# Down product of three MLP groups in four by Strassen's algorithm, weight sums by accumulating DMAs, last norm by column halves

## What is computed

```
for i in range(2):
    h = h + mixer_i(rms_norm(h, norm_mix_g[i]))
    h = h + square(relu(rms_norm(h, norm_mlp_g[i]) @ w_up[i])) @ w_down[i]
return rms_norm(h, norm_final_g)          # h: 512 x 1024
```

## Time and profile before

| | |
|---|---|
| runs, median | 1224.68 us |
| profiled execution, own time | 1224.22 us |
| its span | 1222.5 us |
| PE busy | 1195.8 us (98%), 5821 matmuls |
| DVE busy | 614.3 us (50%) |
| ACT busy | 457.5 us (37%) |
| Pool busy | 41.8 us (3%) |
| DMA | 119.00 MB, mean 97 GB/s |

### The profile page before, as it was taken

How to read it: one execution, slowest core, us unless ns; L and a number is a source line. 1 busy time by engine, 2 the same in 40 slices (tenths; PEclk the granted TensorE clock), 3 DMA queues, 4 the chain that set the end, 5 groups by cost and what they waited for, 6 DMA issues and landing times.

```text
span 1222.5 us, 14644 instructions
## 1 busy us (share of the span) xinstructions
PE 1195.8 (98%) x5821; PEld 1001.4 (82%) x5821; DVE 614.3 (50%) x838; ACT 457.5 (37%) x712; POOL 41.8 (3%) x88
## 2 busy tenths in 40 slices
PE   6999999999999999999999999999999999999996
PEld 5788888888888888888878988987888888888885
DVE  5447878645334344354357666574543433443432
ACT  6346676544223133133345224243531331331421
POOL 2000000000000000000020101100000000000001
PEclk9999999999999999999999999999999999999999
DMA  9245745523233322333211230133322333222101
GB/s 280 65 95 135 161 125 147 192 84 116 93 102 103 103 86 86 103 104 103 84 57 35 70 104 12 59 104 103 121 85 89 102 103 103 90 87 97 34 0 69
DMA packets 115991, 119.00 MB, mean 97 GB/s; under 512 B 38913, under 2 KB 84001, under 8 KB 115938
## 3 DMA queue, kind: packets, MB, share of 16 engines
q1 hardware_dynamic: 112992, 116.47, 31.4%
q10 hardware_dynamic: 2946, 1.79, 0.5%
HBM read 103.50 MB, written 2.10 MB: 86 GB/s over the span
## 4 chain that ended last, share of the span: by engine, by line
PE 95%; DVE 2%; ACT 1%; DMA 1%; issue 1%; POOL 0%; SPq 0%; POOLq 0%; ACTq 0%; DVEq 0%
PE bank L890 15%; PE bank L893 15%; PE bank L894 15%; PE bank L877 10%; PE bank L881 10%; PE bank L880 10%; PE bank L1064 2%; PE bank L1068 2%; PE bank L1067 2%; PE bank L1234 2%; PE bank L1112 2%; PE bank L1099 1%; PE bank L1185 1%; PE bank L1189 1%; PE bank L1188 1%; PE bank L1081 1%
## 5 line engine op out<-in xcount | busy, mean ns | idle before, releaser
L1427 DVE TENSOR_TENSOR w_lo<-w_stage,w_hi 128x2048 fp32r<-128x2048 f32 x87 | 199.9, 2300 | 204.1 <-ACT w_hi L559 204.0
L559 ACT ACTIVATE w_hi<-w_stage 128x2048 fp32r<-128x2048 f32 x87 | 165.9, 1910 | 267.2 <-PE bank L890 213.3
L877 PE MATMUL bank<-hT_lo,w_hi 128*128 128x512 f32 x512 | 199.8, 390 | 0.0
L881 PE MATMUL bank<-hT_hi,w_lo 128*128 128x512 f32 x512 | 199.3, 389 | 0.0
L890 PE MATMUL bank<-w_lo,u_hi 128*128 128x512 f32 x512 | 199.3, 389 | 0.0
L880 PE MATMUL bank<-hT_hi,w_hi 128*128 128x512 f32 x512 | 199.2, 389 | 0.0
L894 PE MATMUL bank<-w_hi,u_lo 128*128 128x512 f32 x512 | 199.2, 389 | 0.0
L893 PE MATMUL bank<-w_hi,u_hi 128*128 128x512 f32 x512 | 199.2, 389 | 0.0
L890 PE MATMUL bank<-w_lo,hT_hi 128*128 128x512 f32 (+1 forms) x320 | 115.1, 360 | 4.4 <-DVE hT_lo L1718 1.9
L1501 DVE TENSOR_TENSOR u_sq<-relu 128x512 f32<-128x512 f32 x64 | 44.3, 692 | 143.2 <-ACT relu L616 143.2
L616 ACT ACTIVATE relu<-bank 128x512 f32<-128x512 f32 x64 | 38.3, 598 | 205.3 <-PE bank L881 205.3
(11 more groups left out here) (206 smaller groups left out, 1513.8 us busy)
## 6 DMA issues: line engine op xcount, KB each, us to landing
w_stage<-in_mlp_w_up_dram SPq DMA_DIRECT2D x32, 1024.0 KB, 5.1
w_stage<-in_mlp_w_down_dram SPq DMA_DIRECT2D x32, 1024.0 KB, 5.0
w_stage<-in_fox_w_in_dram SPq DMA_DIRECT2D x32, 256.0 KB, 4.3
w_stage<-in_gla_w_in_dram SPq DMA_DIRECT2D x8, 1024.0 KB, 5.1
w_stage<-in_fox_w_in_dram SPq DMA_DIRECT2D x4, 1024.0 KB, 8.0
qa<-qk_hi SPq DMA_DIRECT2D x32, 128.0 KB
w_stage<-in_fox_w_out_dram SPq DMA_DIRECT2D x4, 1024.0 KB, 5.2
w_stage<-in_gla_w_in_dram SPq DMA_DIRECT2D x8, 512.0 KB, 4.4
```

The source lines that it names most:

```text
L559: act.activation(w_hi[:, slot, :], w_stage[:, slot, :], ACT.Copy).then_inc(w_hi_made, 1)
L877: a = pe.matmul(out, w[0][:, k, :], x[1][:, k, :], start=(k == 0), stop=False)
L881: a = pe.matmul(out, w[1][:, k, :], x[0][:, k, :], start=False, stop=(k == KT - 1))
L1427: dve.tensor_tensor(w_lo[:, slot, :], w_stage[:, slot, :], fp(w_hi[:, slot, :]), ALU.subtract).then_inc(w_lo_made, 1)
```

## The change

The order of the inner columns is used to cut a group's down product into quadrants. The group's u (512 tokens by 1024 inner columns) is seen as A11, A12, A21, A22 with 256 tokens each and the even or odd tiles of 128 inner columns (four of each); the weights (1024 by 1024) as W11, W12, W21, W22 of 512x512, one unit each. Three groups of four in each layer use seven products in place of eight (Winograd's form of Strassen's algorithm); the fourth is as before.

- The loop has 11 units: U0 to U3 for the up part, then W11, T1 = W11 + W12, T2 = T1 + W22, W22, T3 = W12 + W22, W21, T4 = T2 + W21. T1, T2 and T4 are made one after the other in stage slot 3, T3 in stage slot 1, each by a DMA issued on Pool that adds 1 MB from DRAM to what the slot holds (`weight_sums`). An add in slot 3 is issued when DVE has made the `lo` part of the slot's last value.
- Of u, `u_raw` holds the squares of two k blocks. DVE forms r1 = A21 - A22, s3 = A11 - A21, s2 = r1 - A11, s4 = A12 + s2 (`sums`, 256 columns each). ACT and DVE then make `hi` and `lo` of seven parts of 256 columns at once (`hi`, `lo`); for the fourth block in two pieces: A12, A22, A11 first, then r1, s2, s3, s4. A21 itself is not split.
- A product is 4 k blocks x 2 token blocks x 3 matmuls into two banks (`product`). `begins` is set for three of the seven; the other four go on top of a bank's content once DVE has collected it into `h` (`collect`, scaled by `mlp_scale` or `mlp_minus`). PE's first product waits at its first matmul until three of the four blocks have their `lo` parts, and the first two wait at their fourth k block for the last.
- The squares before the norm, the iota constants and the masks keep their content but move: `xor` and `other` lie in `gate_w`, the masks are made after the third group of layer 0.
- The last norm: ACT's squares of the left half come first, DVE multiplies the left half by the gain (`scale_left`) between the two halves' adds, ACT multiplies by `rstd` (`left`), and DVE does the right half of block t behind the add of block t+1 (`right`). The gain is loaded by ACT into `w_stage` in the last group. The last block is stored in two halves, by ACT and by SyncE.

Constants and order of units:

```diff
-GLA_U = MLP0_U + 8 * GROUPS
+WINO = GROUPS - 1
+WINO_UNITS = 11
+U0, U1, U2, U3, W11, T1, T2, W22, T3, W21, T4 = range(WINO_UNITS)
+HI_SLOT = (0, 1, 3, 1, 2, 0, 1, 2, 0, 1, 2)
+STAGE = (0, 1, 2, 0, 3, 3, 3, 0, 1, 2, 3)
+LEFT_FOR = (W21 - WINO_UNITS, T4 - WINO_UNITS, U0, U2, T4 - WINO_UNITS, U1, W11, T1, T2, W22, T3)
+WINO_LOADS = ((U0, 0, T3 - WINO_UNITS), (U1, 1, T3 - WINO_UNITS), (U2, 2, T4 - WINO_UNITS),
+              (W11, 3, T4 - WINO_UNITS), (U3, 0, U0), (T3, 1, U1), (W21, 2, U2), (W22, 0, U3))
+LOADS_PER_SLOT = (3, 2, 2, 1)
+A_R1, A_S2, A_S3, A_S4, A_12, A_22, A_11, A_21 = range(8)
+PRODUCTS = ((W11, A_11, 4), (T1, A_R1, 6), (T2, A_S2, 4), (W22, A_S4, 6), (T3, A_S3, 4), (W21, A_12, 2), (T4, A_22, 4))
+SUMS = ((0, 0, 1), (2, 1, 1), (0, 1, -1), (0, 1, 1), (2, 1, -1), (0, 0, 1), (2, 0, 1))
+HB = 2 * P
+CLASSIC0_U = MLP0_U + WINO * WINO_UNITS
+GLA_U = CLASSIC0_U + 8
 GLA_OUT_U = GLA_U + 3 * GLA_H
...
```

SyncE's loads and Pool's accumulating DMAs:

```diff
-                    load_rows(g, 8, c + 4, down_d[layer], g * KT)
+                with sp.Fori(0, WINO) as g:
+                    for unit, slot, free in WINO_LOADS:
+                        sp.wait_ge(w_lo_made, g * WINO_UNITS + (c + free + 1))
+                        if unit < 4:
+                            dma = sp.dma_start(cols(w_stage, slot, 256), up_d[layer][:, :, ds(g * D + unit * 256, 256)])
+                        else:
+                            two, half = {W11: (0, 0), T3: (0, 1), W21: (1, 0), W22: (1, 1)}[unit]
+                            dma = sp.dma_start(w_stage[:, slot, :].rearrange("p (k n) -> p k n", k=KT // 2),
+                                               down_pairs_d[layer][:, ds(g * (KT // 2), KT // 2), two,
+                                                                   half * S:(half + 1) * S])
+                        dma.then_inc(w_loaded[slot], 16)
...
@@ -462,7 +534,31 @@
                 pool.wait_ge(squared, n * 2 * TB + TB)
                 step(pool.tensor_tensor(ss[:, 0, :], ss[:, 0, :], ss[:, 1, :], ALU.add))
                 step(pool.tensor_tensor(ss[:, 0, :], ss[:, 0, :], mean_eps[:], ALU.add))
-                pool.tensor_tensor(mlp_scale[:], ss[:, 0, :], minus_one[:], ALU.pow).then_inc(mlp_scale_made, 1)
+                step(pool.tensor_tensor(mlp_scale[:], ss[:, 0, :], minus_one[:], ALU.pow))
+                pool.tensor_tensor(mlp_minus[:], mlp_scale[:], minus_one[:], ALU.mult).then_inc(mlp_scale_made, 1)
+
+            def weight_sums(layer):
+
+                c = (MLP0_U, MLP1_U)[layer]
+
+                def rows(g, two, half):
+                    return down_pairs_d[layer][:, g * (KT // 2):(g + 1) * (KT // 2), two, half * S:(half + 1) * S]
+
+                def add(slot, src, unit):
+                    pool.dma_start(w_stage[:, slot, :].rearrange("p (k n) -> p k n", k=KT // 2), src,
+                                   accum_op=ALU.add).then_inc(t_made[unit], 16)
+
+                for g in range(WINO):
+                    first = c + g * WINO_UNITS
+                    count, per, slot = wino_loaded(layer, T3)
+                    pool.wait_ge(w_loaded[slot], 16 * (g * per + count))
+                    add(1, rows(g, 1, 1), T3)
+                    pool.wait_ge(w_lo_made, first + W11 + 1)
+                    add(3, rows(g, 0, 1), T1)
+                    pool.wait_ge(w_lo_made, first + T1 + 1)
+                    add(3, rows(g, 1, 1), T2)
+                    pool.wait_ge(w_lo_made, first + T2 + 1)
+                    add(3, rows(g, 1, 0), T4)
 
             def gla_norm():
```

ACT's order in a group (`raw` is relu and square in place; `wino_hi` waits for `w_begun` and for the load or the sum):

```diff
+            def wino_hi(layer, g, unit):
+
+                c = (MLP0_U, MLP1_U)[layer]
+                act.wait_ge(w_begun, g * WINO_UNITS + (c + LEFT_FOR[unit] + 1))
+                if unit in (T1, T2, T3, T4):
+                    act.wait_ge(t_made[unit], g * 16 + 16 * (layer * WINO + 1))
+                else:
+                    count, per, slot = wino_loaded(layer, unit)
+                    act.wait_ge(w_loaded[slot], g * (16 * per) + 16 * count)
+                act.activation(w_hi[:, HI_SLOT[unit], :], w_stage[:, STAGE[unit], :], ACT.Copy).then_inc(w_hi_made, 1)
...
+                def raw(g, t):
+
+                    j, to = t // 2, raw_parts(t // 2, *((A_11, A_21 + 1) if t % 2 == 0 else (A_12, A_22 + 1)))
+                    act.wait_ge(up_done, g * 8 + (tiles + t + 1))
+                    if t % 2 == 0 and j > 1:
+                        act.wait_ge(u_lo_made, g * U_PARTS + (parts + j - 1))
+                    act.activation(to, bank[t % 4][:], ACT.Relu).then_inc(relu_made, 1)
+                    act.wait_ge(relu_made, g * 8 + (tiles + t + 1))
+                    act.activation(to, to, ACT.Square).then_inc(u_made, 1)
+
+                def hi(g, j, first, last, of_sums):
+                    if of_sums:
+                        act.wait_ge(s_made, g * 4 + (layer * 4 * WINO + j + 1))
+                    else:
+                        act.wait_ge(u_made, g * 8 + (tiles + 2 * j + 2))
+                    act.activation(u_parts(0, j, first, last), raw_parts(j, first, last), ACT.Copy).then_inc(u_hi_made, 1)
+
+                act.wait_ge(squared, (3 + 4 * layer) * TB)
+                with act.Fori(0, WINO) as g:
+                    wino_hi(layer, g, U1)
+                    wino_hi(layer, g, U2)
+                    raw(g, 0)
+                    raw(g, 1)
+                    hi(g, 0, A_R1, A_11 + 1, True)
+                    raw(g, 2)
+                    raw(g, 3)
+                    wino_hi(layer, g, U3)
+                    hi(g, 1, A_R1, A_11 + 1, True)
+                    wino_hi(layer, g, W11)
+                    raw(g, 4)
+                    wino_hi(layer, g, T1)
+                    raw(g, 5)
+                    hi(g, 2, A_R1, A_11 + 1, True)
+                    raw(g, 6)
+                    raw(g, 7)
+                    hi(g, 3, A_12, A_11 + 1, False)
+                    hi(g, 3, A_R1, A_S4 + 1, True)
+                    for unit in (T2, W22, T3, W21, T4):
+                        wino_hi(layer, g, unit)
...
```

PE's product:

```diff
+                def product(g, n):
+                    unit, part, to = PRODUCTS[n]
+                    split_of(g, WINO_UNITS, c + unit)
+                    if n in (2, 3, 4, 6):
+                        pe.wait_ge(added, g * WINO_ADDS + (adds + {2: 2, 3: 4, 4: 6, 6: 10}[n]))
+                    hi, lo = (b[:, HI_SLOT[unit], :].rearrange("p (k n) -> p k n", k=KT // 2) for b in (w_hi, w_lo))
+                    begins = n in (0, 1, 5)
+                    for k in range(KT // 2):
+                        if n == 0 and k == 0:
+                            pe.wait_ge(u_lo_made, g * U_PARTS + (parts + 3))
+                        if n < 2 and k == 3:
+                            pe.wait_ge(u_lo_made, g * U_PARTS + (parts + 4 + n))
+                        for t in range(2):
+                            xs = [u_parts(b, k, part, part + 1)[:, t * P:(t + 1) * P] for b in range(2)]
+                            out = bank[to + t][:]
+                            a = pe.matmul(out, xs[0], lo[:, k, :], start=(begins and k == 0), stop=False,
+                                          skip_group_check=True)
+                            if k == 0 and t == 0:
+                                a.then_inc(w_begun, 1)
+                            pe.matmul(out, xs[0], hi[:, k, :], start=False, stop=False, skip_group_check=True)
+                            a = pe.matmul(out, xs[1], hi[:, k, :], start=False, stop=(k == KT // 2 - 1),
+                                          skip_group_check=True)
+                            if k == KT // 2 - 1:
+                                a.then_inc(sum_done, 1)
...

```

DVE's order in a group:

```diff
+                def sums(g, j):
+
+                    dve.wait_ge(u_made, g * 8 + (tiles + 2 * j + 2))
+                    r1, s2, s3, s4, a12, a22, a11, a21 = (raw_parts(j, n, n + 1) for n in range(8))
+                    mine.then(dve.tensor_tensor(r1, a21, a22, ALU.subtract))
+                    dve.tensor_tensor(s3, a11, a21, ALU.subtract)
+                    mine.then(dve.tensor_tensor(s2, r1, a11, ALU.subtract))
+                    dve.tensor_tensor(s4, a12, s2, ALU.add).then_inc(s_made, 1)
+
+                def lo(g, j, first, last, part):
+                    dve.wait_ge(u_hi_made, g * U_PARTS + (parts + part))
+                    dve.tensor_tensor(u_parts(1, j, first, last), raw_parts(j, first, last),
+                                      fp(u_parts(0, j, first, last)), ALU.subtract).then_inc(u_lo_made, 1)
+
+                def collect(g, n):
+
+                    first, half, sign = SUMS[n]
+                    if n == 3:
+                        dve.wait_ge(added, g * WINO_ADDS + (adds + 6))
+                    for t in range(2):
+                        dve.wait_ge(sum_done, g * WINO_ADDS + (adds + 2 * n + t + 1))
+                        to = h[:, first + t, half * S:(half + 1) * S]
+                        scale = (mlp_scale if sign > 0 else mlp_minus)[:, first + t:first + t + 1]
```

(118 more changed lines are left out.)

256 lines of the change are left out of this document (140 added, 116 removed).

## The result

The change makes the kernel slower: 1240.78 us (median of 4 runs, 1240.04 to 1243.23) against 1224.78 us; the ratio is 1.0128 (95% interval 1.0103 to 1.0153). The forecast was 1217, range 1205 to 1239. L, the time of the DMA add, came out as rival (a) has it, 8.6 us with stalls of 6.4 us. But for stalls of 6.4 us rival (a) gives 1227 us; the 14 us above that come from a loss that neither the forecast nor any rival had, the clock of TensorE.

What follows compares the result with a forecast made beforehand. PE was taken as the bound (98% of the span). From 1224.2 us, 32.6 for matmuls and 3.3 for the last norm came off, and six stalls of 6.6 - 1.9 were added: 1216.5, 1217 on the median; range 1205 to 1239.

Steps and rivals of the forecast that it cites:

- rival (a): In each Strassen group, T1's add takes 8.3 to 12 us, stalls 6.4 to 10.1, total 1227 to 1256; chance 0.32.
- I take 6.6: T1's accumulating DMA on Pool: 6.6 us from issue to landing, its two read streams overlapping in part.
- full second pass: In the accumulating DMA: reading the destination adds 3.0 us to the plain load's 5.0, giving 8.0 us.
- PE waits L - 1.9 us in each of the six groups: Before product W11: PE stalls for the DMA add's issue-to-landing time less 1.9 us; 4.7 a group, 28 in six.
- the walk: One new group's ACT, DVE and PE queues timed from up tile 0; PE's first product, due at 43.5 us, waits for lo(2).
- Removed matmuls, 32.6 us: Down part of six groups: 168 matmuls for 192, 144 fewer in all at unchanged price, saving 32.6 us.
- Last norm, -3.3 us: At the kernel's end: multiplying by halves lets adds keep PE's pace, saving 3.3 us (bounds 2 and 4).
- Edits at nothing: Splits in a layer's first group, moved masks, Pool's extra norm operation, T3's accumulate and later products: nothing, or to 0.2 us.
- Rival (c): Before the first product: chain shorter than walked or absorbed by PE, stall 2 us or less, total 1189 to 1201; chance 0.07.
- Rival (d): Down products: bank-collect waits hold PE once per product, 9 us on top, 1226; no chance of its own.

Runs made afterwards that it cites:

- t1_behind_tile6: Changed kernel with T1's hi queued behind raw 5, hi(2) and raw 6 on ACT, and T1's lo behind sums(2) and lo(2) on DVE; 1230.69 us.
- w11_early: Changed kernel with W11 split right behind U2 at the group's start, and T1's add issued by Pool before T3's; 1193.84 us, ratio to before 0.9742.
- w11_early_t2_first: As w11_early, with T2's hi and lo before those of the fourth block's last four parts; 1190.28 us, ratio 0.9712.
- wait_by_block: Changed kernel where PE's first product waits for the third k block's lo only at that block, 12 matmuls later; 1226.39 us.

## Why the prediction was wrong, step by step

- *"I take 6.6"* for L failed by size. It is 8.6 us. The transfer itself is 3.0 us of sixteen engines for a copy; for the add, by windows over one (columns as above),

```profile
298.00:299.00 1.00, 1.00 (x6) 0.80 (x6) 0.00 (x0) 0.00 (x0) 0.26 (x1) 1.00 0.16 6
299.00:300.00 1.00, 1.00 (x6) 0.85 (x5) 0.00 (x0) 0.00 (x0) 0.00 (x0) 1.00 0.88 78
300.00:301.00 1.00, 1.00 (x7) 0.81 (x6) 0.00 (x0) 0.00 (x0) 0.00 (x0) 1.00 1.09 199
...
303.00:304.00 1.00, 1.00 (x6) 0.82 (x5) 0.00 (x0) 0.00 (x0) 0.00 (x0) 1.00 1.16 213
304.00:305.00 1.00, 1.00 (x6) 0.84 (x5) 0.00 (x0) 0.00 (x0) 0.00 (x0) 1.00 0.82 148
```

the DMA share sums to 6.3 us over 298 to 306, at some 200 GB/s. That is the full second pass, 8.0 by the prediction's own bound, and 0.6 more. I argued that the read of the destination would overlap in part with the read of DRAM; the doubled busy time says that it does not. The rule of the Trainium skill that the prediction quotes ("Collectives: The Full Stack", on the bandwidth ceiling) agrees with this trace: twice the busy time. It should have been the forecast, not the rival. The stall came to 38.3 us against 28.2, 10 of the 24 us of error, and that alone turns the forecast's gain of 8 us into a loss of 2.
- *"PE waits L - 1.9 us in each of the six groups"* held: 6.7 by the formula, 6.4 measured, six times, before W11, released by the lo of the third block. t1_behind_tile6 and w11_early moved and removed it as the walk says. Apart from L I priced the chain right, and never asked what stands first in it.
- *The clock* is the term that was missing: the sum "1224.2 - 32.6 - 3.3 + 6 x (6.6 - 1.9) = 1216.5" has nothing for it. Every sum, and every rival, treated a waiting PE as lost time and no more. It costs 11 to 14 us in the four kernels with six long gaps (their rest less the 2 us of the others), 1.8 to 2.3 a gap; it is the other 14 us of error here with the 2 us of rest, and it is why the time lies above the upper end of the range: 1224.2 - 35.9 + 38.3 = 1226.6 without it. The Trainium skill ("TensorE: Matmul & The Clock Gate", section on HAM oscillation) warns of idle gaps that throttle the clock and make the next work start cold; the windows above agree. The page of before shows the clock at 9 in every slice, but finer windows of the same trace do show the effect, at 832 to 836 (0.52 and 0.63, 1.7 us lost behind a wait of 1.9 us, above). Six such losses would have put 10 us into the sum before the run.
- *Removed matmuls, 32.6 us*: right. 144 fewer at the unchanged cadence; w11_early_t2_first comes to 1190.3 against 1188.3.
- *Last norm, -3.3 us*: right on DVE's chain, 2.9 us by the medians.
- *Edits at nothing* (U1 in a layer's first group, masks, Pool's extra operation, T3, W22, W21, T4): right; none has a wait in the changed kernel's list.
- *Rival (c)*, a stall of 2 us or less, was wrong for this order of work and becomes true when W11's split and T1's add are moved forward (w11_early, 0.5 us). *Rival (d)* had no part: PE's waits have no row before any other product. *Rival (a)* had L and the stall right and lacked the clock, so that the measured 1240.8 lies in its range of times, 1227 to 1256, is in part luck.

## What to carry to other kernels

A gap of PE can cost its length and then a slow restart: six gaps of 3.7 us cost about as much clock as six of 6.4, six of 0.5 none, and one of 1.9 cost some in four executions of nine. So split a wait's price into length and number. Shortening the six gaps from 6.4 to 3.7 us gave back only length (14.4 us), filling them only clock (10.7 us), abolishing them both (50.5 us from 1240.8 to 1190.3). Look for a half clock in windows of a few microseconds: a slice of a fortieth of the span hides it. When work is exchanged for a chain through other engines and a DMA, ask first when its first link could start at the earliest, and only then what its links cost: W11 lay in its slot since the group's start, and its split waited behind work that didn't need it. A change that measures slower can still be a good one in a bad order: the same seven products, with the same last norm, are 3% faster than before, or 1% slower.

## What the runs showed of the hardware that I had not expected

- A DMA that adds 1 MB from DRAM into SBUF, 512 rows of 2 KB, issued by Pool, takes 8.6 us to land; the same as a copy 5.9; issued by SyncE 5.0 in the kernel before and 5.8 beside Pool's copies. Pool is busy 1.28 to 1.50 us with issuing an add, 0.75 to 0.95 us with a copy (layer 0's first group).
- The clock can fall after PE is back at work (in wait_by_block PE is back at 403.24, and the clock is 1.00 up to 403.90 and 0.50 from 404.00), so a gap that ends with the clock still at 1.00 isn't yet free.
- A wait of 1.9 us was enough for the clock to fall in the kernel before (0.52 at 832 to 834), in some executions and not in others.
- After a gap PE ran 3.7 to 6.2 us at half the clock; the length differs between gaps of the same kernel.
